# Level masks one step earlier, a store behind two loads, and x turned by a diagonal of reciprocal roots

## The reference, cut to what matters

```python
h = _rms(x, norm_g[i])                 # x * rsqrt(mean(x*x) + eps) * g
u = h @ w_in[i]                        # 13312 columns
# columns of u: HGRN2 recurrence (q, i, forget forward, forget backward, gate),
# neighbourhood attention (q, k, v, gate), two merge gates
oa = _hgrn2_bidir(hq, hi, hf_fwd, hf_bwd, lower[i, 0], lower[i, 1])
...
    o_inter = jnp.einsum('bhtk,bhkv->bhtv', qb * jnp.exp(b), state)
    decay = jnp.exp(jnp.where(tri[:, :, None], diff, NEG))
    att = jnp.einsum('bhtk,bhsk,bhtsk->bhts', qb, kb, decay)
    o_intra = jnp.einsum('bhts,bhsv->bhtv', att, vb)
...
y = jax.nn.sigmoid(m_a) * ya + jax.nn.sigmoid(m_b) * yb
x = x + y @ w_out[i]
g = jax.nn.sigmoid(_rms(x, ple_norm[i]) @ w_ple_gate[i])
x = x + (p[i] @ w_ple[i]) * g
```

## Time and profile before

| what | value |
| --- | --- |
| median of 3 runs | 1824.24 us |
| the profiled execution, device time | 1823.45 us |
| its span, first to last instruction | 1821.7 us |
| PE busy | 1783.3 us (98%) |
| PE weight loads busy | 1531.3 us (84%) |
| DVE busy | 1186.1 us (65%) |
| ACT busy | 837.8 us (46%) |
| POOL busy | 202.4 us (11%) |
| granted TensorE clock, mean | 1.000 |

### The profile page before, as it was taken

The page is one execution under the profiler, slowest core; times in us unless marked ns, Lnnn a source line. Parts: engine busy times, 40 slices in busy tenths (PEclk is TensorE's granted clock), DMA queues, the critical chain, the costliest instruction groups (busy, mean ns, idle before and its releaser), DMA issues.

```text
span 1821.7 us, 24066 instructions
## 1 busy us (share of the span) xinstructions
PE 1783.3 (98%) x9337; PEld 1531.3 (84%) x9337; DVE 1186.1 (65%) x1408; ACT 837.8 (46%) x1133; POOL 202.4 (11%) x205
## 2 busy tenths in 40 slices
PE   6999999999999999999999999999999999999998
PEld 5899999888788888888888888888888888888887
DVE  6977777778587878787787878784444422244332
ACT  7444444434375747474746565655222232243221
POOL 4000000000040404040303131320000000000000
PEclk9999999999999999999999999999999999999999
DMA  7243344576633332323233333335545544465331
GB/s 226 90 136 116 117 150 149 173 253 195 175 96 94 95 100 86 99 86 110 86 97 88 104 92 101 95 110 156 151 140 150 167 150 160 165 228 189 122 121 71
DMA packets 287661, 240.89 MB, mean 132 GB/s; under 512 B 9657, under 2 KB 233944, under 8 KB 286032
## 3 DMA queue, kind: packets, MB, share of 16 engines
q1 hardware_dynamic: 284096, 227.59, 40.6%
q0 software_dynamic: 3472, 12.05, 1.9%
HBM read 210.80 MB, written 28.80 MB: 132 GB/s over the span
## 4 chain that ended last, share of the span: by engine, by line
PE 70%; DVE 14%; ACT 10%; issue 5%; DMA 2%; SPq 0%; ACTq 0%; DVEq 0%
PE mm_ps L1870 7%; PE mm_ps L1872 7%; PE mm_ps L1871 6%; PE mm_ps L2095 5%; PE mm_ps L2096 5%; PE mm_ps L2094 5%; PE ax_ps L1857 2%; PE ax_ps L1859 2%; PE ax_ps L1858 2%; PE ax_ps L1872 2%; PE ax_ps L1871 2%; PE ax_ps L1870 2%; DVE w_lo L344 2%; DVE dif L1477 2%; PE ax_ps L2096 2%
## 5 line engine op out<-in xcount | busy, mean ns | idle before, releaser
L344 DVE TENSOR_TENSOR w_lo<-w_raw,w_hi 128x1024 fp32r<-128x1024 f32 (+1 forms) x200 | 271.9, 1360 | 373.6 <-ACT w_hi L335 373.4
L335 ACT ACTIVATE w_hi<-w_raw 128x1024 fp32r<-128x1024 f32 (+1 forms) x200 | 228.1, 1141 | 476.2 <-PE ax_ps L2096 208.0
L1870 PE MATMUL mm_ps<-act_hl,w_hi 128*128 128x512 f32 x960 | 383.1, 399 | 1.4 <-DVE w_lo L344 1.4
L1872 PE MATMUL mm_ps<-act_hl,w_lo 128*128 128x512 f32 x960 | 374.7, 390 | 0.0
L1871 PE MATMUL mm_ps<-act_hl,w_hi 128*128 128x512 f32 x960 | 374.2, 390 | 0.0
L1872 PEld LDWEIGHTS mm_ps<-act_hl,w_lo 128*128 128x128 f32 x960 | 180.2, 188 | 38.8
L1870 PEld LDWEIGHTS mm_ps<-act_hl,w_hi 128*128 128x128 f32 x960 | 180.4, 188 | 37.3 <-issue 1.8
L1871 PEld LDWEIGHTS mm_ps<-act_hl,w_hi 128*128 128x128 f32 x960 | 180.5, 188 | 36.0
L963 ACT ACTIVATE q_hi<-q_raw 128x1024 fp32r<-128x1024 f32 x84 | 87.5, 1057 | 141.7 <-DVE q_raw L1320 81.3
L2094 PE MATMUL mm_ps<-w_hi,act_hl 128*128 128x512 f32 x384 | 149.8, 390 | 0.0
L2096 PE MATMUL mm_ps<-w_lo,act_hl 128*128 128x512 f32 x384 | 149.4, 389 | 0.0
(11 more groups left out here) (299 smaller groups left out, 3773.6 us busy)
## 6 DMA issues: line engine op xcount, KB each, us to landing
w_raw<-in_w_in SPq DMA_DIRECT2D x120, 512.0 KB, 3.8
q_raw<-in_w_in SPq DMA_DIRECT2D x56, 512.0 KB, 5.6
r_in<-in_w_in SPq DMA_DIRECT2D x56, 512.0 KB, 4.6
w_raw<-in_w_ple_gate SPq DMA_DIRECT2D x20, 768.0 KB, 4.3
w_raw<-in_w_out SPq DMA_DIRECT2D x16, 768.0 KB, 4.3
w_raw<-in_w_branch_a SPq DMA_DIRECT2D x16, 512.0 KB, 3.7
w_raw<-in_w_branch_b SPq DMA_DIRECT2D x16, 512.0 KB, 3.7
g_ab<-gate_dram SPq DMA_DIRECT2D x14, 512.0 KB, 4.1
```

The lines of the kernel that those rows point to most:

```text
L335: nc.scalar.activation(w_hi[:, s, 0:width], w_raw[:, s, 0:width], ACT.Copy).then_inc(hi_done, 1)
L344: nc.vector.tensor_tensor(w_lo[:, s, 0:width], w_raw[:, s, 0:width], w_hi[:, s, 0:width].bitcast(F32), ALU.subtract).then_inc(lo_done, 1)
L1870: MM(bank, wh, m_hi[:, k0 + k, :], start=start and k == 0, stop=False)
L1872: mm = MM(bank, wl, m_hi[:, k0 + k, :], start=False, stop=stop and k == kn - 1)
```

## The change

Three parts.

**x is turned by a product.** DVE no longer scales x. It multiplies the 128x128 identity by the reciprocal roots, one per row, into `x_diag[:, t, :]`, and PE multiplies the raw piece of x by this diagonal, which turns and scales it at once. PE's operation is an ordinary float32 product and no longer a transpose. The first four pieces are turned for token group 0 as soon as its diagonal is there, and then for group 1. Group 3's root stands ahead of piece 11 instead of 12.

**A store.** The store of piece 1 of the last value group moves behind the first two weight loads of head 0.

**The masks.** DVE's copies of levels 0 and 1 move from step 13 to step 12, for each of the eight heads.

```diff
+            x_diag = sb("x_diag", [P, NT, P], where=first)
...
-        START_SPLIT, START_ROOT = {0: 0, 8: 1, 24: 2}, {4: 2, 12: 3}
+        START_SPLIT, START_ROOT = {0: 0, 8: 1, 24: 2}, {4: 2, 11: 3}
...
                     if j == 16:
                         store_rows(g, 0)
-            store_rows(GROUPS - 1, 1)
-
...
                     load_w(sp, us, i, win_v[:, 8 * (i % 2):8 * (i % 2) + 8, bass.ds(h * P + COL[TILES[i // 2]], P)])
+                    if i == 1 and h == 0:
+                        store_rows(GROUPS - 1, 1)
                     if i == 2 and h == 0:
                         store_rows(GROUPS - 1, 2)
...
-                TS(x_in[:, t, :], x_in[:, t, :], stat[:, 2, t:t + 1], None, ALU.mult).then_inc(x_normed, 1)
+                if t == 0:
+                    dve.wait_ge(pool_step, 2)
+                TS(x_diag[:, t, :], ident[:, :], stat[:, 2, t:t + 1], None, ALU.mult).then_inc(x_normed, 1)
...
-                    if i == 13:
+                    if i == 12:
                         level_products(h, 0)
                         level_products(h, 1)
...
+            def turn_tokens(n, t):
+
+                k, half = n % KT, n // KT
+                return MM(ax_ps[:, n % 5, t * P:(t + 1) * P], x_in[:, 2 * half + t, k * P:(k + 1) * P],
+                          x_diag[:, 2 * half + t, :], start=True, stop=True)
+
             def turn_h(n):
...
                 for t in range(2):
-                    mm = nc.tensor.transpose(ax_ps[:, n % 5, t * P:(t + 1) * P],
-                                             x_in[:, 2 * half + t, k * P:(k + 1) * P], ident[:, :])
+                    mm = turn_tokens(n, t)
                 mm.then_inc(h_turned, 1)

             def first_tile():

-                for n in range(4):
-                    turn_h(n)
+                for t in range(2):
+                    pe.wait_ge(x_normed, t + 1)
+                    for n in range(4):
+                        mm = turn_tokens(n, t)
+                        if t == 1:
+                            mm.then_inc(h_turned, 1)
```

More of the change, by code:

```diff
@@ L1793, in _ @@
             MM = nc.tensor.matmul
+            def turn_tokens(n, t):
+                k, half = n % KT, n // KT
+                return MM(ax_ps[:, n % 5, t * P:(t + 1) * P], x_in[:, 2 * half + t, k * P:(k + 1) * P],
+                          x_diag[:, 2 * half + t, :], start=True, stop=True)
             def turn_h(n):
-                k, half = n % KT, n // KT
+                half = n // KT
                 pe.wait_ge(x_normed, 2 * half + 2)
```

## The result

| | before | after |
| --- | --- | --- |
| median | 1823.64 us (4 runs, 1822.47 to 1824.29) | 1809.71 us (4 runs, 1808.58 to 1810.05) |
| the profiled execution, device time | 1823.45 us | 1809.62 us |
| its span | 1821.7 us | 1807.9 us |
| PE busy | 1783.3 us (98%) | 1789.1 us (99%) |
| DVE busy | 1186.1 us | 1176.8 us |

The ratio is 0.9923, 95% interval 0.9906 to 0.9940: 13.9 us faster (forecast 12.3 faster, 1812), within the range. The table's "before" is measured beside the changed kernel, with one more run than the three of the front.

A forecast was written before the change was run, and what follows sets the result against it. PE, busy 98% of the span, was taken as the bound, so only its waits and work count: 1823.45 - 12.2 (masks) - 1.4 (store) + 1.3 (turn of x) = 1811.2 us, forecast as a median of 1812, range 1809 to 1814, 1808 to 1817 with rivals.

The forecast's parts named there:

- The masks, 12.2 us: Heads: level copies moved ahead of the squares, `n_q` and a weight unit remove PE's eight waits, gaining 12.2 us.
- The tie at the mean of squares: Each head: the diagonal copy still ends as before, so PE reaches the mean of squares with 0.04 us to spare.
- The rival of POOL's traffic: Heads: copies stretched beside POOL's additions; 1816 to 1820 us (chance 0.08), or past 1.6 us slower, 1831 (0.04).
- The store, 1.4 us: Head 0's first loads: issued 3.3 us earlier, `w_lo` done about 2.9 us earlier, PE's 1.4 us wait gone.
- A product is two instructions at 0.11 us: Stage 1: a product costs two transposes of 0.11 us each, adding 7.1 us of work to PE over 64 turns.
- The rival of four transposes: Stage 1: a product costs 0.44 us, stage ends at 54.3, kernel 1825 us; chance 0.05 shared with an ineffective mask edit.
- The walk of stage 1, 40.8 us: Stage 1: PE starts group 1 at 13.9, full pace at 18.0, ends at 40.8 instead of 39.50, costing 1.3 us.
- The diagonal, 0.2 us: Stage 1: making a diagonal costs DVE 0.2 us instead of 1.29 us scaling a group.
- The start keeps its waits: Stage 1 rival: PE still waits 1.2 and 1.6 us, the turn costs 4.1 us, time 1815 us; chance 0.08.
- The rival of an early full pace: Stage 1: group 0's early products bring full pace sooner; stage costs 0.2 to 0.7 us, time 1811; chance 0.05.

The follow-up runs named there:

- experiment 1: Only the level copies moved from step 13 to 12, against the kernel before: 1808.7 us, ratio 0.9921.
- experiment 6: Changed kernel with the backward diagonal copy moved behind the low part of step 14's weight unit: 1816.69 us, 7.0 us slower than the changed kernel.
- experiment 7: Changed kernel with the level copies behind the squares and `n_q` but ahead of step 13's weight unit: 1814.11 us, 4.4 us slower than the changed kernel.
- experiment 2: Only the store moved behind head 0's first two weight loads, against the kernel before: 1821.66 us, ratio 0.9990.
- experiment 5: Changed kernel with raw x turned by transposes against the identity, scaling left out: 1806.33 us, 3.4 us less than the changed kernel.
- experiment 9: Changed kernel with 21 filler products of the identity in PE's idle start: 1808.12 us, ratio to the kernel before 0.9923.
- experiment 3: Only x turned by the diagonal, group 3's root at piece 11, against the kernel before: 1826.72 us, ratio 1.0016.
- experiment 10: Changed kernel with the diagonal for only 8 of 64 turns, the rest scaled and transposed, plus 21 filler products in PE's idle start: 1806.29 us, ratio to the kernel before 0.9911.

## Why the prediction was right

The mechanism was right in all three parts, and the sum was 1.6 us short of the gain. Most of this is the masks, which gave 1.7 us more than their term. Luck enters in stage 1, whose end moves by about 1 us between executions with the time at which PE's pace rises. By its steps:

- **The masks, 12.2 us: right in kind, too small.** Measured 13.9 (experiment 1 and the changed kernel alike). The term was the sum of listed waits; each is 0.15 us short from start to start, and the first products behind a pause are 0.08 us longer.
- **The tie at the mean of squares: mis-sized, on the safe side.** I put the margin at 0.04 us, arguing that the order of the same instructions can't move the end of the last. It can: the squares need 0.58 us less away from POOL's stretch, and the copies, put into it, only 0.05 us more, in all eight heads alike. The prediction had the squares' 1.25 us in a rival and left it out of this sum. The margin is 0.58 us; experiment 6 used it up and then paid 0.93 a head.
- **The rival of POOL's traffic: refuted.** 1.60 us for the pair, against 1.55; it would have needed 1.6 us more. Experiment 7 shows the other half, 1.26 us for the squares left where they were. The 1.22 us that this rival quotes for `w_lo` is that of head 0's first weight unit and not of a row unit; the comparison holds, since units of that shape take 1.21 away from POOL here.
- **The store, 1.4 us: right.** 1.5 (experiment 2); again the listed wait was a little short.
- **A product is two instructions at 0.11 us: right**, by 0.80 us a piece and by experiment 5. The rival of four transposes (54.3 us for the end of stage 1) is out. There the Trainium skill, TensorE: Matmul & The Clock Gate, section Terms, gives a factor of four for FP32 transposes; the time here agrees with two.
- **The walk of stage 1, 40.8 us: right on the mean, by luck in part, with one wrong step.** Group 1's start was put at 13.9 and the first projection product at 16.3; they came at 13.80 and 16.38. Full pace was put at 18.0, by adding the 4.1 us of the earlier trace rows to the earlier start. That doesn't hold: four executions of the same start reached it at 19.3, 19.4, 18.0 and 17.5 us, and ended at 41.17, 41.34, 40.55 and 40.24, on the mean 40.83. Four of the old order ended at 39.50, 39.55, 39.01 and 39.52, on the mean 39.40. The turn thus costs 1.4 us there, in one execution between 0.7 and 1.8. The rest of the walk holds: 16.38 + 23.4 + half of the 2.84 us up to the clock's rise at 19.22 is 41.20, measured 41.17, so the 0.2 us for ACT's roots weren't needed. With full pace throughout it is 40.09 (experiment 9), near the 39.7 to 39.9 that the walk gives.
- **The diagonal, 0.2 us: 0.29.** It starts group 1 where it was reckoned.
- **The start keeps its waits: refuted.** The 1.6 us on `act_hl` and the 1.2 us at a later turn are gone. The 1.18 us now listed ahead of group 1 are idle time at the start, between the two groups, as in the walk.
- **The rival of an early full pace:** full pace came at 19.3 us in the changed kernel, with products, at 19.5 in experiment 5, with transposes, and at 19.2 before. So group 0's products alone didn't bring it; it came earlier in two executions of four for no reason that the order of instructions gives. Experiment 9 shows that early work can bring it, when there is more of it. The Trainium skill, TensorE: Matmul & The Clock Gate, Part 4: PE-mode transpose, would let products bring it and not transposes; these three times don't show that, and projection products stand among the transposes in each.

The whole, in the profiled executions: -13.9 us over the heads (the first level products at 532.7 before and 533.2 after, the last run that waited at 1198.8 before and 1185.4 after), +1.7 in stage 1, +0.4 at the late load, -1.5 at the store, -0.5 elsewhere: -13.8. Of the last, 0.4 lie at the turn in stage 4 that experiment 3 shortens as well.

## What to carry over

A wait in the list is priced from start to start: from the last instruction ahead of it to the first behind it, in both orders. Here the list was 14% short. When instructions on one engine are reordered beside another engine's stretch, ask for each whether it is one of those that the stretch lengthens: here moving a copy from PSUM in and an addition of SBUF rows out gained time. An operation can be folded into PE where that opens an idle start, but only for the pieces that PE would otherwise wait for: eight turns of 64 gave the early start, and with the other 56 turned by transposes stage 1 ended 2.9 us earlier (38.29 for 41.17). A head shown by itself should be laid beside the other seven: in experiment 7 the third one waited almost twice as long as most.

## What the runs showed of the hardware

- Beside POOL's additions the squares (two inputs from SBUF, 128x512) took 1.25 us and 0.67 away from them, `w_lo` (two inputs from SBUF, 128x1024) 1.53 and 1.21, but the pair of predicated copies from PSUM 1.60 and 1.55 to 1.60. POOL's three additions took 3.67 us beside `w_lo` and squares and 3.23 beside `w_lo` and copies.
- The view of the granted clock doesn't show the slow pace at the start: it reads 1.00 (2.4 GHz) in every stretch from 2 us on, while the same product takes 0.41 us and later 0.28. The packed trace has no entry of the clock ahead of the rise. Its first entry says 2.4 GHz and lies at 19.13 us before, 19.22 in the changed kernel, 5.65 in experiment 9 and 7.02 in experiment 10, where the lengths of the rows change; without an entry the view prints 1.00. A fall behind the first entry does show, as experiment 10's 0.50 from 14 to 16 us, with the same length (eight instructions in 2.08 us) as the start of the changed kernel. So the slow start is taken to be the clock of 1.2 GHz, and in it only the lengths of the rows tell.
- The time of the rise differed by 2.2 us between four executions of one order of instructions (17.3 to 19.5 us by the clock's entries; 18.9 to 20.3 in four of the old order), and 18 products of nothing in the idle start brought it to 5.65 us. The pace outlasted pauses of 2.20 and 1.53 us in one kernel and was lost in another behind pauses of 2.44 and 1.20 us, one execution each.
